# Two transformer blocks on one core: in the second block, a branch's norm and the next norm from one round of sums, and the residual addition on GpSimd

## The reference

```
def rms_norm_2(x, g):
    y = x * lax.rsqrt(jnp.mean(x * x, axis=-1, keepdims=True) + 1e-6)
    return y * g

x = rms_norm(x) * final_norm                     # end of the first block
mem_n = rms_norm_2(mem, mem_norm)
for i in range(2):
    g = ln_gains[i]
    hn = rms_norm_2(x, g[0])
    t = rglru_mixer(hn, ...) if i == 0 else rwkv7_mixer(hn, ...)
    x = x + rms_norm_2(t, g[1])
    c = mem_cross_attention(rms_norm_2(x, g[2]), mem_n, ...)
    x = x + rms_norm_2(c, g[3])
    m = sqrelu_mlp(rms_norm_2(x, g[4]), ...)
    x = x + rms_norm_2(m, g[5])
```

## Time and profile before

| | us |
|---|---|
| median of three runs | 2564.89 |
| runs | 2560.28, 2564.89, 2569.64 |
| profiled execution | 2560.17 |
| its span, first to last instruction | 2558.2 |
| busy TensorE, weight loads, VectorE, ScalarE, GpSimd | 2265.9, 1994.7, 1647.0, 1153.2, 173.1 |
| mean granted TensorE clock | 0.929 |

### The profile page before, as it was taken

The page is one execution under the profiler, slowest core; times in us unless marked ns, Lnnn a source line. Parts: engine busy times, 40 slices in busy tenths (PEclk is TensorE's granted clock), DMA queues, the critical chain, the costliest instruction groups (busy, mean ns, idle before and its releaser), DMA issues.

```text
span 2558.2 us, 40095 instructions
## 1 busy us (share of the span) xinstructions
PE 2265.9 (89%) x16364; PEld 1994.7 (78%) x16364; DVE 1647.0 (64%) x2514; ACT 1153.2 (45%) x2008; POOL 173.1 (7%) x153
## 2 busy tenths in 40 slices
PE   3999998889999999887999897979969698897997
PEld 3888977778878888776887797668858697766886
DVE  5886667678778775656775665367464653535764
ACT  3554344455455443444654463345434311334542
POOL 0110022001001001110110000000000040000000
PEclk9999898989999998898999798989979798998998
DMA  7776743357757666324666253436635000442663
GB/s 276 269 249 211 266 152 113 99 182 270 247 213 267 239 223 229 102 76 132 214 223 189 85 164 115 122 119 188 190 105 160 23 4 2 132 124 75 190 184 104
DMA packets 113797, 417.07 MB, mean 163 GB/s; under 512 B 12624, under 2 KB 12880, under 8 KB 113104
## 3 DMA queue, kind: packets, MB, share of 16 engines
q1 hardware_dynamic: 112752, 409.56, 48.2%
q10 hardware_dynamic: 864, 4.96, 0.5%
HBM read 413.42 MB, written 1.05 MB: 162 GB/s over the span
## 4 chain that ended last, share of the span: by engine, by line
PE 81%; DVE 11%; ACT 5%; issue 3%; DMA 1%; POOL 0%; DVEq 0%; ACTq 0%; POOLq 0%
PE banks L476 80%; ACT weight_upper L1947 1%; DVE weight_lower L1277 1%; ACT heap L2051 1%; DVE weight_ring L1288 1%; DVE heap L1354 1%; DVE heap L1588 1%; ACT heap L2126 0%; DVE heap L1623 0%; PE banks L806 0%; DVE nmax L1464 0%; DVE heap L1462 0%; DVE xn_t L1567 0%; DVE heap L1696 0%; DVE diag L1332 0%
## 5 line engine op out<-in xcount | busy, mean ns | idle before, releaser
L476 PE MATMUL banks<-xn_halves,weight_upper 128*128 128x512 f32 (+1 forms) x3552 | 1036.4, 360 | 45.1 <-DVE weight_lower L1277 32.7
L1277 DVE TENSOR_TENSOR weight_lower<-weight_ring,weight_upper 128x1024 fp32r<-128x1024 f32 x580 | 723.8, 1253 | 372.5 <-ACT weight_upper L1947 370.6
L476 PE MATMUL banks<-xn_halves,weight_lower 128*128 128x256 f32 x2832 | 814.3, 288 | 31.3 <-DVE branch_a_lower L1499 13.0
L1947 ACT ACTIVATE weight_upper<-weight_ring 128x1024 fp32r<-128x1024 f32 x580 | 608.5, 1054 | 343.3 <-PE banks L476 240.0
L476 PEld LDWEIGHTS banks<-xn_halves,weight_upper 128*128 128x128 f32 x3552 | 645.2, 197 | 146.8 <-DVE weight_lower L1277 33.3
L476 PEld LDWEIGHTS banks<-xn_halves,weight_lower 128*128 128x128 f32 x2832 | 553.4, 195 | 40.0 <-DVE branch_a_lower L1499 15.0
L476 PE MATMUL banks<-hidden,weight_upper 128*128 128x512 f32 x1216 | 422.3, 392 | 5.7 <-DVE heap L1375 4.2
L476 PE MATMUL banks<-hidden,weight_lower 128*128 128x256 f32 x1216 | 339.9, 280 | 0.0
L476 PEld LDWEIGHTS banks<-hidden,weight_upper 128*128 128x128 f32 x1216 | 228.3, 188 | 57.2 <-DVE heap L1375 5.2
L476 PEld LDWEIGHTS banks<-hidden,weight_lower 128*128 128x128 f32 x1216 | 228.3, 188 | 0.0
L1288 DVE CUSTOM_DVE_ANT_0 weight_ring<-weight_ring,c_rows,vecs 128x1024 f32<-128x1024 f32 x144 | 187.2, 1302 | 26.1 <-DMA weight_ring<-w_ada_dram 24.4
(11 more groups left out here) (256 smaller groups left out, 2429.2 us busy)
## 6 DMA issues: line engine op xcount, KB each, us to landing
weight_ring<-w_ada_dram SPq DMA_DIRECT2D x144, 512.0 KB, 4.4
weight_ring<-ffn_gate_dram SPq DMA_DIRECT2D x88, 512.0 KB, 3.6
weight_ring<-ffn_up_dram SPq DMA_DIRECT2D x88, 512.0 KB, 3.8
weight_ring<-ffn_down_dram SPq DMA_DIRECT2D x88, 512.0 KB, 3.5
weight_ring<-m_w_up_dram SPq DMA_DIRECT2D x64, 512.0 KB, 3.6
weight_ring<-m_w_down_dram SPq DMA_DIRECT2D x64, 512.0 KB, 3.6
weight_ring<-w_in_dram SPq DMA_DIRECT2D x58, 512.0 KB, 3.9
weight_ring<-b_w_rkv_dram SPq DMA_DIRECT2D x24, 512.0 KB, 3.6
```

The costliest lines, as they stand in the source:

```text
L476: return nc.tensor.matmul(o, w, r, start=first, stop=last)
L1277: V.tensor_tensor(w_lo[:, n % RING, :], ring[:, n % RING, :], w_hi[:, j % SPLITS, :].bitcast(F32), ALU.subtract).then_inc(*did("weight_low ...
L1947: A.activation(w_hi[:, j % SPLITS, :], ring[:, n % RING, :], ACT.Copy).then_inc(*did("weight_upper", j))
```

## The change

At a join the program now forms three sums while the branch's outputs arrive: A of the squares of t, C of t times gain times X (new on VectorE, L1611 of the new file), B of the squares of gain times t (new on ScalarE). The sum of squares of the new X is then the old one of X plus 2 r C plus r squared B, r being the branch's rstd; the norm behind it needs no pass over X. The sum of X's own squares is carried from join to join. GpSimd adds slices 1 to 6 of each sum (`sums`, L2420) and later adds t to X (`added`, L2427), while VectorE scales four slices ahead and makes xn between (`joined`). Behind the first block there are A and B, and no X is added; at the end only A. Everywhere, also in the first block, ScalarE takes the root from the sums with 1/n and epsilon in one instruction, and the spread has the broadcast column as weights and the identity as the moving side: the means and diagonals go. The memory's norm moves behind the input projections of the recurrent branch, its load to another place; the output is stored in four parts.

```diff
+SUM_A, SUM_B, SUM_C, PART, SUM_X, ROOT, RSTD, RSTD_X = range(8)
...
+def sum_tile(n, what, f):
+    if what == SUM_A:
+        return (sq if n == 6 else t_sq)[:, f, :]
+    at = min(f, 1) + (f - 1) % 3 * (f > 0)
+    if n == 6:
+        return latent_n[:, at, :]
+    x = slot[10] if n[1] == 5 else slot[8]
+    return x[:, (4 if what == SUM_C else 0) + at, :]
...
+def sums_of(n):
+    return (SUM_A, SUM_B) if n == 6 else (SUM_A,) if n == (DEPTH - 1, 5) else (SUM_A, SUM_C, SUM_B)
...
+SUM_DONE = {SUM_A: "squares", SUM_B: "gain_squares", SUM_C: "with_x"}
...
-    sp.wait_ge(*of("x_final", ((DEPTH - 1, 5), KD - 1)))
-    sp.dma_start(out, X[:, :, :]).then_inc(*did("out_stored", 0, by=16))
-    sp.wait_ge(*of("out_stored", 0))
+    for j in range(KD // 2):
+        sp.wait_ge(*of("x_added", ((DEPTH - 1, 5), 2 * j + 1)))
+        sp.dma_start(out[:, 2 * j:2 * j + 2, :], X[:, 2 * j:2 * j + 2, :]).then_inc(
+            *did("out_stored", j, by=16))
+    sp.wait_ge(*of("out_stored", KD // 2 - 1))
...
-        pe.wait_ge(*of("rstd_diag", n))
+        pe.wait_ge(*of("rroot", n))
...
-            mn = mm(cols(4, P, t * P), ones, diag[:, t, :], True, True)
+            mn = mm(cols(4, P, t * P), root[:, 2, t:t + 1].broadcast_to((P, P)), ident, True, True)
...
+    def mix_sums(n):
+        refill(4, 5)
+        for part in range(2):
+            for what in sums_of(n):
+                f = (KD - 1) * part
+                if part:
+                    pe.wait_ge(*of(SUM_DONE[what], (n, f)))
+                else:
+                    pe.wait_ge(*of("sum_added", (n, what, KD - 2)))
+                for t in range(QT):
+                    mn = mm(bank[:, 4 + t, 3 * part + what:3 * part + what + 1],
+                            sum_tile(n, what, f)[:, t * P:(t + 1) * P], ones[:, 0:1], True, True)
+        mn.then_inc(*did("square_sums", n))
+        readers[4] = readers[5] = [("mix_sums", n)]
...
+    def spread_two(n, n2):
+        for m, which, b in ((n, RSTD, 6), (n2, RSTD_X, 7)):
+            if m is not None:
+                refill(b)
+                pe.wait_ge(*of("rroot", m))
+                for t in range(QT):
+                    mn = mm(cols(b, P, t * P), mix_stat[:, which, t:t + 1].broadcast_to((P, P)), ident,
+                            True, True)
+                mn.then_inc(*did("rstd", m))
+                readers[b] = [("rstd_read", m)]
...
-    spread(6)
...
-    for k in range(KD):
-        squares_sum((0, 0), k, KD)
+    spread_two(6, (0, 0))
...
-        spread((i, 0))
...
+        squares_of_two("mem")
+        spread("mem")
...
-        spread((i, 1))
-        squares_of_two((i, 2))
+        spread_two((i, 1), (i, 2))
...
-        spread((i, 5))
-        if i + 1 < DEPTH:
-            squares_of_two((i + 1, 0))
+        spread_two((i, 5), (i + 1, 0) if i + 1 < DEPTH else None)
...
-    def rstd(n, cnt=D):
-        dve.wait_ge(*due("square_sums", n))
-        for t in range(QT):
-            last = V.tensor_scalar(root[:, 0, t:t + 1], bank[:, 4 + t, 0:1], 1.0 / cnt, EPS,
-                                   ALU.mult, ALU.add)
-            last.then_inc(*did("mean", (n, t), also=[("mean_square", n)] if t else []))
+    def rstd(n, w=QT):
...
-        V.reciprocal(root[:, 2, 0:2], root[:, 1, 0:2]).then_inc(*did("rroot", n))
-        dve.wait_ge(*due("rroot", n))
-        for t in range(QT):
-            V.tensor_scalar(diag[:, t, :], ident, root[:, 2, t:t + 1], None,
-                            ALU.mult).then_inc(*did("diag", (n, t), also=[("rstd_diag", n)] if t else []))
+        V.reciprocal(root[:, 2, 0:w], root[:, 1, 0:w]).then_inc(*did("rroot", n))
...
+    def mem_normed():
+        for k in range(KD):
+            V.scalar_tensor_tensor(mem_n[:, k, :], mem_n[:, k, :], vec("mem_norm", k), cols(4), ALU.mult,
+                                   ALU.mult).then_inc(
+                *did("normed2", ("mem", k), also=[("rstd_read", "mem")] if k == KD - 1 else []))
...
+    def mixed(s, n, gain):
+        for f in range(KD + 1):
+            if f < KD:
+                dve.wait_ge(*due("mixed_half", (s, f)))
+                V.tensor_tensor(t_out[:, f, :], cols(held["down_raw", (s, f)]), t_out[:, f, :], ALU.add
+                                ).then_inc(*did("mixed", (s, f)))
+            if f and SUM_C in sums_of(n):
+                dve.wait_ge(*due("mixed", (s, f - 1)))
+                if f > 4:
+                    dve.wait_ge(*due("sum_added", (n, SUM_C, f - 4)))
+                V.scalar_tensor_tensor(sum_tile(n, SUM_C, f - 1), t_out[:, f - 1, :], gain(f - 1),
+                                       X[:, f - 1, :], ALU.mult, ALU.mult).then_inc(
+                    *did("with_x", (n, f - 1)))
...
+    def joined(n, n2, gain, gain2=None, parts=True):
+        src = X if n == 6 else t_out
+        ready = "mixed_n" if n == 6 else "x_added"
...
+        def scaled(k):
+            V.scalar_tensor_tensor(src[:, k, :], src[:, k, :], gain(k), cols(6), ALU.mult,
+                                   ALU.mult).then_inc(
+                *did("mixed_n", (n, k), also=[("rstd_read", n)] if k == KD - 1 else []))
...
+        dve.wait_ge(*due("square_sums", n))
+        step(V.tensor_reduce(stat_of(SUM_A, 3), bank[:, 4:6, 0:6].rearrange("p t (m w) -> p w t m", m=2),
+                             AX.X, ALU.add), [("mix_sums", n)])
+        dve.wait_ge(*due("root", n))
+        V.reciprocal(stat_of(RSTD), stat_of(ROOT)).then_inc(*did("rroot", n))
+        if n2 is not None:
+            dve.wait_ge(*due("rroot", n))
+            step(V.tensor_tensor(stat_of(PART), stat_of(SUM_B), stat_of(RSTD), ALU.mult))
+            if n != 6:
+                step(V.scalar_tensor_tensor(stat_of(PART), stat_of(SUM_C), 2.0, stat_of(PART),
+                                            ALU.mult, ALU.add))
+            step(V.tensor_tensor(stat_of(PART), stat_of(PART), stat_of(RSTD), ALU.mult))
+            if n != 6:
+                step(V.tensor_tensor(stat_of(PART), stat_of(PART), stat_of(SUM_X), ALU.add))
+            step(V.tensor_scalar(stat_of(SUM_X), stat_of(PART), 0.0, None, ALU.max), [("mean_square", n2)])
+            dve.wait_ge(*due("root", n2))
+            V.reciprocal(stat_of(RSTD_X), stat_of(ROOT)).then_inc(*did("rroot", n2))
+        dve.wait_ge(*due("rstd", n))
+        early = KD // 2 if n2 is not None else KD
+        for k in range(early):
+            scaled(k)
+        if n2 is not None:
+            dve.wait_ge(*due("rstd", n2))
+            for k in range(KD + 1):
+                if k < KD:
+                    dve.wait_ge(*due(ready, (n, k)))
+                    V.scalar_tensor_tensor(xn[:, k, :], X[:, k, :], gain2(k), cols(7), ALU.mult,
+                                           ALU.mult).then_inc(
+                        *did("normed2", (n2, k), also=[("rstd_read", n2)] if k == KD - 1 else []))
+                    if k + early < KD:
+                        scaled(k + early)
+                if k and parts:
+                    lower(xn_hl, k - 1, xn[:, k - 1, :], ("normed_upper", (n2, k - 1)),
+                          ("normed_lower", (n2, k - 1)))
...
+        for k in range(1, KD - 1):
+            squares_add("mem", k)
+        rstd("mem")
+        dve.wait_ge(*due("rstd", "mem"))
+        mem_normed()
...
-    gained("mem", slot[10], mem_n, lambda k: vec("mem_norm", k), False)
-    rstd((0, 0))
+    joined(6, (0, 0), lambda k: vec("final_norm", k), ln(0, 0))
...
-        gained((i, 0), X, xn, ln(i, 0), i == 0)
...
-        mixed((i, 0), (i, 1))
-        rstd((i, 1))
-        added((i, 1), ln(i, 1))
-        for k in range(1, KD - 1):
-            squares_add((i, 2), k)
-        rstd((i, 2))
-        gained((i, 2), X, xn, ln(i, 2), True)
+        mixed((i, 0), (i, 1), ln(i, 1))
+        joined((i, 1), (i, 2), ln(i, 1), ln(i, 2))
...
+        mixed((i, 1), (i, 3), ln(i, 3))
+        joined((i, 3), (i, 4), ln(i, 3), ln(i, 4))
...
-        mixed((i, 2), (i, 5))
-        rstd((i, 5))
-        added((i, 5), ln(i, 5), "x_added" if i + 1 < DEPTH else "x_final")
+        mixed((i, 2), (i, 5), ln(i, 5))
...
-            for k in range(1, KD - 1):
-                squares_add((i + 1, 0), k)
-            rstd((i + 1, 0))
+            joined((i, 5), (i + 1, 0), ln(i, 5), ln(i + 1, 0), False)
+        else:
+            joined((i, 5), None, ln(i, 5))
...
+    def gain_square(n, f, src, gain):
+        if f > 3:
+            act.wait_ge(*due("sum_added", (n, SUM_B, f - 3)))
+        A.activation(sum_tile(n, SUM_B, f), src, ACT.Square, scale=gain).then_inc(
+            *did("gain_squares", (n, f)))
...
-    def root_of(n, w=2):
-        act.wait_ge(*due("mean_square", n))
-        A.activation(root[:, 1, 0:w], root[:, 0, 0:w], ACT.Sqrt).then_inc(*did("root", n))
+            if n == 6:
+                gain_square(n, k, X[:, k, :], vec("final_norm", k))
...
+    def root_of(n, counts=(D,)):
+        act.wait_ge(*due("square_sums", n))
+        for c, cnt in enumerate(counts):
```

(48 more changed lines are left out.)

120 lines of the change are left out of this document (36 added, 84 removed).

## The result

The changed kernel took **2525.2 us** in the median of four runs (2512.1 to 2527.0), the kernel before, beside it, 2562.6 (2557.2 to 2569.6). The ratio is **0.9845**, with a 95% interval of 0.9808 to 0.9881: 1.5% faster, 37 us. The profiled execution of the changed kernel is its fastest one: 2512.1, span 2510.3, 12 to 15 us under the other three.

What follows compares the result with a forecast made beforehand. TensorE's work plus its waits were taken to bound the kernel. Gains of 13, 5.7, 19.1, 2.2 and 3.0 sum to 43.0 us, from 2560.2 (profiled) or 2564.9 (median) to 2520; range 2495 to 2545.

Steps and rivals of the forecast that it cites:

- the four joins: Second block, behind down projections with 8 chunks: restart of TensorE 3.3 us earlier at each, 13 in all.
- (0,5): Join behind the MLP's down projection with 32 chunks: restart 20.9 us after its last matmul against 26.6, gaining 5.7.
- the first join: End of the first block, three norms in a row: 24.1 us gained, 2.1 and 2.9 given back, net 19.1.
- Last addition, T0+7.7: Joins behind 8 chunks: GpSimd's last addition ends 7.7 us after the last down matmul, held up by VectorE.
- Rival A: At the joins GpSimd keeps up: last addition 3.1 us after the last down matmul, total 2501 us; chance 0.20.
- Mean addition 0.74 to 0.8: GpSimd's additions at the joins: a mean near 0.74 to 0.8 us each when blocked little.
- Rival B: GpSimd loses the port at the joins: 2582 us at full price, gain used up at mean addition 1.23; chance 0.07.
- The sums behind the last addition, 3.6: Joins: TensorE's sixteen rows of 128x1 sums behind GpSimd's last addition take 3.6 us at the low clock.
- S to the restart, 6.0: Joins behind 8 chunks: from sums done (S) to the first projection 6.0 us, the first subtraction waiting for GpSimd.
- What is given back behind it: Behind the first block: convolution chain 2.1 us later, last gate of the recurrent branch 2.9 later.
- rival C: First join gives less: convolution and gates late by twice the count, later joins 2 less each, 2533 us; chance 0.15.
- Norms of the first block, 3.0: First block: six times the diagonal goes from a place where TensorE waits, 3.0 us gained.

Runs made afterwards that it cites:

- run 1: Changed kernel with VectorE's weight splits reading one SBUF tile, the weights' lower halves zero; single time 2478.2 us, not comparable.
- run 2: Changed kernel with the sums' additions at the second block's joins on VectorE in place of GpSimd; 2505.8 us, ratio to before 0.9789.
- run 3: Changed kernel with each join's eight residual additions to X back on VectorE, sums still on GpSimd; 2539.6 us, ratio to before 0.9919.
- run 7: Changed kernel with sums on VectorE, plus filler matmuls where TensorE waits in a join; 2505.1 us, ratio to before 0.978.
- run 9: The kernel of run 6 with VectorE's subtraction moved ahead of the scaling in the loop behind a join; 2493.9 us, ratio to before 0.9729.
- Run 4: Changed kernel with the six additions of the memory's squares on GpSimd in place of VectorE; 2516.9 us, ratio to before 0.9835.
- runs 10 to 12: No edit: two more profiles of the kernel before, one of the changed kernel; first block's last matmul ends at 1399.7, 1400.6 and 1409.2 us.
- run 6: Changed kernel with sums on VectorE, one slice fewer added there and summed by TensorE, memory's squares on GpSimd; 2493.3 us, ratio to before 0.9732.

## Why the prediction was right, step by step

**The time.** 2520 was forecast, 2525.2 came, in the range, from the case it had called likeliest. That it came so near is in part luck: the gains of the joins and the cost behind the first block were both sized too small, and the first block's gain had the wrong sign. By the landmarks the four joins gave 19.0 (forecast 13), (0,5) 5.9 (5.7), the first join 14.9 (19.1), the end 2.4 (2.2); the stages between took 2.3 more (0), the first block 4.6 more (3.0 less). That makes 35, where 43 was forecast.

- **Waits and what bounds the kernel**: right. The waits of the earlier trace rows were what could be had.
- **Last addition, T0+7.7**: it was T0+5.7 at (0,1). The mechanism was right, one port that one engine at a time holds for a whole operation, and so was the start (T0-13.2 against T0-13.1). The mis-sized term is the addition on the port. The product holds it for 0.28, as I said, the split for 1.08 (I said 1.1), but I gave an addition its whole duration, 0.74; it ends 0.60 behind the operation that it waited for, and 0.68 behind another addition. Of the 18.9 us that the 18 took, 7 x 0.28 and 5 x 1.08 leave 0.64 for each; with that my count of 20.8 would have been 19.0. Rival A (T0+3.1) needed no collision; run 1 nearly gives it by making VectorE's part shorter, run 2 by leaving GpSimd out.
- **Mean addition 0.74 to 0.8**: wrong, 1.00 over all 108 and 1.05 in the joins, since the duration of a blocked addition has the wait in it. The median is 0.748, the highest 1.735: the median hides the collision. Rival B decided at 1.23 and was not so far.
- **The sums behind the last addition, 3.6**: 4.0. **S to the restart, 6.0**: 6.1, in all four joins; in the experiments too (6.1 to 6.4), but for run 3 (8.3, additions to X ahead) and three joins of run 7 (6.8 to 7.0, fillers ahead). That the first subtraction waits there for a GpSimd addition is what run 9 shows.
- **(0,5)**: 20.8 against 20.9; last addition at T0+3.5 (3.6), sums at T0+7.3 (7.2). With no split beside it the last pair of additions took 1.58, with one beside it 2.42.
- **End of the first block**: gap 8.85 against 8.6.
- **What is given back behind it**: 9.8, not 5.0. The late convolution (1.7, forecast 2.1) was right. The step that failed is "VectorE's additions and eight scalings of the memory (3.1) lie in its waits before the first gate": the additions come right behind the convolution, where TensorE is waiting for the next split. (The prediction's 3.1 doesn't agree with the 5.4 of its own bound; the additions alone took 3.07.) TensorE takes up its work at restart+43.9 in place of +39.8, of which 2.4 are these additions, and the clock falls behind the longer wait: 0.76 in 1450 to 1456, about 1.6 more (estimate). Run 4 takes both away. The memory's own sums, wait and spread between 1464.2 and 1467.6 take 3.3 to 3.4, near the 2.9 forecast; 0.7 of the 9.8 I leave unassigned. It is half of rival C: the stage came later by twice what I counted, the joins behind it gave no less for it.
- **The end**: about 2.4 to 2.9 against 2.2; the additions took 5.49 against 5.9. Run 3, with them on VectorE, ends as early (2540.0 - 2527.1 = 12.9).
- **Norms of the first block, 3.0**: TensorE's waits for them did fall, from 9.2 to 6.1 in six, but the block didn't get shorter (runs 10 to 12). Why the attention stages behind the shorter waits take up to 10 us more in most executions stays open. The granted clock there is 0.90 in the first profile of after and 0.88 in the second (243 to 535), which names the place and not the cause.
- **No change of the clock**: nearly. In the mean over the joins behind 8 chunks, all profiles, the low clock lasts 4.8 us into the restart, 4.0 before: 0.4 us a join. Run 7 takes it out of the restart, but no time was gained by it.
- **The Trainium skill**, SBUF — State Buffer, section Who interferes with whom: that VectorE with two SBUF inputs contends with a GpSimd instruction that reads SBUF, and that one blocks the other wholly, is borne out by the rows of (0,1): no operation ends sooner than 0.28, 0.60 or 1.08 behind the one that it waited for. That fewer microseconds came out (3.15 per output against 3.6) is no sharing; an addition holds the port for less than it lasts.

That the change gains is shown; that GpSimd is the right engine for its sums is refuted by run 2.

## What to carry to other kernels

Before work moves to an idle engine, count what the busy engine reads beside it, and take an operation's price under a collision from the ends of neighbours, not from durations: here three additions took 3.15 us on idle GpSimd and 1.09 on busy VectorE, while the addition to X, whose neighbours on VectorE read PSUM, was rightly moved. Place small work by the instruction that another engine waits for, not by the engine's idle share: six additions in the one place where TensorE waited cost 3.8 us, a drop of the clock among them. And take landmarks (end of work, restart) from several profiles: gaps of one kernel repeated to 0.3 us here, all but one, while totals of the same code scattered by 15. Even a gap has parts that scatter, the sums with the clock, and parts that don't.

## What the runs showed of the hardware

- GpSimd's addition of 128x256 and a VectorE operation with two SBUF operands don't run side by side: the one that waits ends 0.60 (addition), 0.28 (128x256 on VectorE) or 1.08 (128x1024 on VectorE) behind the end of the other (changed kernel, joins).
- A VectorE operation with one SBUF operand (128x1024, 0.69 alone) is blocked too: 1.0 to 1.1 beside GpSimd's additions, its end 0.55 behind theirs (run 1); I had taken one operand as harmless. VectorE's scalings with an operand in PSUM stayed at 0.39 apart beside GpSimd's additions to X, and those at 0.68.
- The granted clock falls not only when TensorE idles: it fell from 1.00 to 0.50 while TensorE worked through 36 sums of 128x1 without a gap (0.80 in the mean, run 6 at (0,3)). It doesn't always: 24 such sums behind four fillers ran at 1.00 at (1,3) of run 7. It came back under 128x256 fillers, 1.4 us ahead of the restart (run 7, (0,3)).
